# Sample attention: the value page becomes the stationary operand, 16 weight columns move, and all pages add up in one PSUM bank

## The chip, the cores and the metric

One core of a Trainium2 chip runs the whole kernel in one launch. The metric is the device time in microseconds, the median of several executions. All data is fp32; the large projections are made of three fp32r matmuls on split operands.

## What is computed

The kernel is one inference step of a two-layer decoder for a prompt of 512 tokens and for 8 samples of 4 new tokens each. Layer 0 is a recurrent block, layer 1 a stick-breaking attention block. For the samples the attention also reads 1,024 past positions, 8 pages of 128 for each sample, out of a paged pool:

```
past_v = cache_v[page_table].reshape(Bs, n_pages * PAGE_SIZE, KV_HEADS, HEAD_DIM)

z = einsum('bqkgd,bskd->bkgqs', qb, k) / sqrt(HEAD_DIM) + bias
mask = kpos[None, :] < qpos[:, None]
log_keep = where(mask, log_sigmoid(-z), 0.0)
suffix = cumsum(log_keep, axis=4, reverse=True) - log_keep
attn = where(mask, exp(log_sigmoid(z) + suffix), 0.0)
o = einsum('bkgqs,bskd->bqkgd', attn, v)
```

There are 16 query heads in 4 groups (KV_HEADS = 4), of 128 dimensions. So for one sample and one key head 16 columns (4 query heads by 4 tokens) meet a key page and a value page of 128 positions by 128 dimensions. The suffix sum runs backwards over positions, so pages are taken from the newest to the oldest.

## The kernel before

Five engines run programs of their own, written out in the order in which they execute, and meet at semaphores. TensorE's program is: transposes of the input, layer 0 (`block_a`, `pair_b`), the prompt's attention between the projections of layer 1 (`pair` with `qk`, `later`, `rest`, `pv`), then the sample attention, which is the stage of this change, and then the output projection (`pair_e`), whose first weights are loaded before the sample attention begins.

The sample attention goes in steps n = 0 to 8: step 0 is the new tokens themselves (keys `KST`, values `VST`), steps 1 to 8 are one page of each of the 8 samples. In step n TensorE does, in this order (`d_step`):

- for b = 0 to 7 (the sample), `d_turn` transposes the four heads of its key page into a bank of `PS` (L860), a copy by ACT (even b, L1205) or DVE (odd b, L1676) takes it to `KPT`, and four matmuls of 16 moving columns make the scores in `Z` (L878). The transposes run two or three samples ahead, so a step begins with 12 of them and ends with three samples' scores in a row;
- `d_values(n - 1)`: the values of the step before (L851). The weights of one sample (64 columns: 4 key heads by 16) are the stationary operand and the whole value page, 512 columns of 4 heads by 128 dimensions, moves. The result is 64 rows by 512 columns in bank `d_bank(b)` of `PS`. Each row meets all four heads, and only one in four of the blocks is wanted;
- `d_rest_keys(n - 1)` and `d_later_keys(n)`: 512-column matmuls with a triangle of ones, which carry the suffix sum in `later_sum` (L837, L838, L832, L833).

Meanwhile DVE and ACT turn the scores of step n into the exponent (`d_chain`, `d_exps`). DVE has another task in between: `add_values` adds each of the eight banks to an accumulator in SBUF (`value_sums`: `OA` for samples 0 to 5, two pieces of `T` for 6 and 7; L1632). POOL clears these accumulators ahead of the stage. Since key transposes and values share the four banks of `PS`, both wait for these adds (`d_sum_b`). After step 8, 32 transposes turn the accumulators (L900), and DVE multiplies the wanted blocks into the gate (L1684).

SP loads the pages, `KPG` and `VPG`, into two slots; a value slot is free when the matmuls that read it have ended (`d_pv_b`).

Of the kernel before, what the change touches and what calls it, by code (L numbers as in the profile page):

```python
# [26 lines left out]
ALU = mybir.AluOpType  # L27
# [6 lines left out]
NB, NT = 8, 4  # L34
# [10 lines left out]
DH = 128  # L45
NH, NKV, GRP = 16, 4, 4
KVW = NKV * DH
PAGE = 128
NPAGE = 8
# [53 lines left out]
def build(nc, a, out):  # L103
    ctx = ExitStack()
    with ctx:
        def sem(name):
            return ctx.enter_context(nc.semaphore(name))
# [4 lines left out]
        def sb(name, shape, dt=F32, offset=None):  # L112
            size = 4
            for n in shape[1:]:
                size *= n
            if offset is None:
                offset = at[0]
                at[0] += (size + 31) // 32 * 32
            return nc.alloc_sbuf_tensor_at(name, list(shape), dt, offset=offset), offset


        U, U_AT = sb("U", [P, 40, TOK], F32R)
        Y, Y_AT = sb("Y", [P, KR, TOK])
        raw, _ = sb("raw", [P, 2, UT, P])
        WS, _ = sb("WS", [P, 2, 2, UT, P], F32R)
        GW, GW_AT = sb("GW", [P, 2, 2, BLK])
        GWS, GWS_AT = sb("GWS", [P, 2, 2, 2, BLK], F32R)
        T, T_AT = sb("T", [P, 12, 572])
        RS, _ = sb("RS", [P, TOK])
        CH, _ = sb("CH", [P, KR, CROWS])  # L130
# [17 lines left out]
        VPG, _ = sb("VPG", [P, 2, NB, KVW], offset=U_AT + 2 * NB * KVW * 4)  # L148
        KPT, _ = sb("KPT", [P, 4, KVW], offset=U_AT + 4 * NB * KVW * 4)


        OA, _ = sb("OA", [NKV * GRP * NT, 6, KVW], offset=U_AT + (4 * NB + 4) * KVW * 4)

        YO, _ = sb("YO", [P, 5, D], offset=U_AT)

        xin, _ = sb("xin", [P, 5, D], offset=Y_AT)
# [59 lines left out]
        kp_odd = sem("kp_odd")  # L216
        kp_used = sem("kp_used")
        d_mask = sem("d_mask")
        d_cleared = sem("d_cleared")
        d_z = sem("d_z")  # L220
        d_zout = sem("d_zout")
        d_l = sem("d_l")
# [5 lines left out]
        d_rest = sem("d_rest")  # L228
        d_exp = sem("d_exp")
        d_at = sem("d_at")  # L230
        d_pv_b = sem("d_pv_b")
        d_sum_b = sem("d_sum_b")
        d_turned = sem("d_turned")
        d_out = sem("d_out")
        x_in = [sem(f"x_in{t}") for t in range(5)]
        rows_in = sem("rows_in")
# [43 lines left out]
        block = ctx.enter_context(nc.Block())  # L280

        QR = NKV * GRP * NT

        def value_sums(b):
            return OA[:, b, :] if b < 6 else T[0:QR, 5 if b == 6 else 8, 0:KVW]

        def d_columns(tile):

# [6 lines left out]
        def d_bank(b):  # L295

            return PS[:, b % 4 // 2, b % 2, :]
# [26 lines left out]
        def _(sp):  # L324
# [123 lines left out]
            def load_step(n, slot, reused):  # L448

                load_pages(n, slot, KPG, a["cache_k"], keys_in, (kp_t, n * 8 - 16) if reused else None)  # L450
                load_pages(n, slot, VPG, a["cache_v"], values_in, (d_pv_b, n * 8 - 8) if reused else None)

            load_step(1, 1, False)
            load_step(2, 0, False)
# [26 lines left out]
        def _(pool):  # L481
# [89 lines left out]
                ins = pool.affine_select(out=m8[:, k], in_=m8[:, k], compare_op=ALU.is_ge, fill=0.0, base=0,  # L571
                                         pattern=[[-NT, NB], [0, GRP], [0, NT]], channel_multiplier=1)
            ins.then_inc(d_mask, 1)

            pool.wait_ge(pv_done, NH * 4)
            pool.wait_ge(q_low, NH)
            pool.memset(OA[:], 0.0)
            for b in (6, 7):
                ins = pool.memset(value_sums(b), 0.0)
            ins.then_inc(d_cleared, 1)  # L580

            for n in range(2):
                add_square(3 * KD + n, n, 3, n == 0)
# [6 lines left out]
        def _(pe):  # L590
# [249 lines left out]
            def d_values(n, slot, pages=None):  # L840

                if isinstance(n, int) and n == 0:
                    pe.wait_ge(d_at, 1)
                else:
                    pe.wait_ge(d_exp, n + 1)
                    pe.wait_ge(values_in[slot], pages)
                for b in range(NB):
                    if b >= 4:
                        pe.wait_ge(d_sum_b, n * 8 + (b - 3))
                    v = VST[:, :] if isinstance(n, int) and n == 0 else VPG[:, slot, b, :]  # L850
                    ins = pe.matmul(d_bank(b)[0:QR, :], T[:, 4, b * QR:(b + 1) * QR], v, start=True, stop=True)  # L851
                    ins.then_inc(d_pv_b, 1)

            def d_turn(n, slot, b, first):
                if not first and b < 2:
                    pe.wait_ge(d_sum_b, n * 8 - 8)
                if not (first and b < 4):
                    pe.wait_ge(kp_odd if b % 2 else kp_even, n * 4 + (b // 2 - 5))
                for k in range(NKV):
                    ins = pe.transpose(d_bank(b)[:, k * P:(k + 1) * P], KPG[:, slot, b, k * DH:(k + 1) * DH], IDN[:])  # L860
                ins.then_inc(kp_t, 1)
# [31 lines left out]
                d_step(i * 2 + 1, 1, i * PAGES + PAGES, i * PAGES)  # L893
            d_step(NPAGE, 0, NPAGE // 2 * PAGES, NPAGE // 2 * PAGES)
            d_values(NPAGE, 0, NPAGE // 2 * PAGES)

            for b in range(NB):
                pe.wait_ge(d_sum_b, (NPAGE + 1) * NB)
                for k in range(NKV):
                    ins = pe.transpose(d_bank(k)[:, b * QR:(b + 1) * QR], value_sums(b)[:, k * DH:(k + 1) * DH], IDN[0:QR, 0:QR])  # L900
            ins.then_inc(d_turned, 1)


            def pair_e(i, first):
# [25 lines left out]
        def _(act):  # L930
# [248 lines left out]
            def d_exps(n, rows):  # L1179
                q = slice(0, SEQ)  # L1180
                act.wait_ge(d_zout, n + 1)
                if not (isinstance(n, int) and n == 0):
                    act.wait_ge(d_sp, n)
                steps.done(nc.scalar.activation(T[0:rows, 1, q], T[0:rows, 0, q], ACT.Abs))
                steps.done(nc.scalar.activation(T[0:rows, 1, q], T[0:rows, 1, q], ACT.Exp, scale=-1.0))
                nc.scalar.activation(T[0:rows, 1, q], T[0:rows, 1, q], ACT.Ln, bias=1.0).then_inc(d_l, 1)
                act.wait_ge(d_sp, n + 1)
                if isinstance(n, int) and n == 0:
                    act.wait_ge(pv_done, 64)
                else:  # L1190
                    act.wait_ge(d_rest, n)
                nc.scalar.activation(KVP[:, 0, :], T[:, 2, q], ACT.Copy).then_inc(d_high, 1)
                act.wait_ge(d_arg, n + 1)
                if not (isinstance(n, int) and n == 0):
                    act.wait_ge(d_pv_b, n * 8)
                nc.scalar.activation(d_weights(rows), d_columns(T[0:rows, 3, q]), ACT.Exp).then_inc(d_exp, 1)  # L1196

            d_exps(0, NS)
# [37 lines left out]
        def _(dve):  # L1236
# [388 lines left out]
            head_out(*last_head)  # L1625


            def add_values(m, sequences):

                for b in sequences:  # L1630
                    dve.wait_ge(d_pv_b, m * 8 + (b + 1))
                    V.tensor_tensor(value_sums(b), value_sums(b), d_bank(b)[0:QR, :], ALU.add).then_inc(d_sum_b, 1)  # L1632

            def d_chain(n, par, rows):
                q = slice(0, SEQ)
                fresh = isinstance(n, int) and n == 0
                if fresh:
                    dve.wait_ge(d_z, 1)
                else:
                    dve.wait_ge(kp_used, n * 8)  # L1640
                    dve.wait_ge(d_l, n)
                V.scalar_tensor_tensor(T[0:rows, 0, q], Z[0:rows, 0, par, :], SCALE, T[0:rows, 6, q],
                                       ALU.mult, ALU.add).then_inc(d_zout, 1)
                if not fresh:
                    add_values(n - 1, range(0, 4))
                dve.wait_ge(d_l, n + 1)
                steps.done(V.scalar_tensor_tensor(T[0:rows, 2, q], T[0:rows, 0, q], 0.0, T[0:rows, 1, q], ALU.max, ALU.add))
                if fresh:
                    steps.done(V.tensor_tensor(T[0:rows, 3, q], T[0:rows, 0, q], T[0:rows, 2, q], ALU.subtract))
                    dve.wait_ge(d_mask, 1)  # L1650
                    V.tensor_tensor(T[0:rows, 2, q], T[0:rows, 2, q], T[0:rows, 7, q], ALU.mult).then_inc(d_sp, 1)
                else:
                    V.tensor_tensor(T[0:rows, 3, q], T[0:rows, 0, q], T[0:rows, 2, q], ALU.subtract).then_inc(d_sp, 1)
                if not fresh:
                    add_values(n - 1, range(4, 5))
                dve.wait_ge(d_high, n + 1)
                V.tensor_tensor(KVP[:, 1, :], T[:, 2, q], KVP[:, 0, :].bitcast(F32), ALU.subtract).then_inc(d_low, 1)
                if not fresh:
                    add_values(n - 1, range(5, 8))
                dve.wait_ge(d_later, n + 1)  # L1660
                V.tensor_tensor(T[0:rows, 3, q], T[0:rows, 3, q], later_sum[0:rows, :], ALU.subtract).then_inc(d_arg, 1)
                if fresh:
                    dve.wait_ge(d_exp, 1)
                    V.tensor_tensor(d_weights(rows), d_weights(rows), d_columns(T[0:rows, 7, q]), ALU.mult).then_inc(d_at, 1)

            d_chain(0, 0, NS)
            dve.wait_ge(d_cleared, 1)
            with dve.Fori(0, NPAGE // 2) as i:
                steps.loop(i, 0, 2)
                for m in (1, 2):  # L1670
# [5 lines left out]
                        V.tensor_copy(KPT[:, b % 4, :], d_bank(b)).then_inc(kp_odd, 1)  # L1676
                    d_chain(n, m % 2, P)
            steps.leave(NPAGE // 2)
            add_values(NPAGE, range(NB))
            dve.wait_ge(d_turned, 1)  # L1680
            for k in range(NKV):
                y = Y[:, k * GRP:(k + 1) * GRP, SEQ:TOK].rearrange("p g (b t) -> p g b t", t=NT)
                o = d_bank(k).rearrange("p (b k g t) -> p k g b t", b=NB, k=NKV, g=GRP)[:, k]
                ins = V.tensor_tensor(y, y, o, ALU.mult)  # L1684
            ins.then_inc(d_out, 1)

# [56 lines left out]
```

## Time and profile before

| | |
|---|---|
| median of 3 runs | 2100.48 us (2094.29 to 2105.5) |
| profiled execution | span 2086.1 us; its own time is not among those listed |
| TensorE matmul busy | 1896.6 us, 91% of the span |
| DVE busy | 1143.1 us, 55% |
| ACT busy | 787.0 us, 38% |
| mean granted TensorE clock | 0.92 of full speed |
| from 1596 to 1840 us (sample attention but its start) | granted clock 0.75 on average |

The span runs from the first to the last instruction of the one execution that was profiled. The granted clock is a share of TensorE's full speed of 2.4 GHz; 0.50 is 1.2 GHz. Matmul records overlap, since they are pipelined: the mean duration of one is longer than the distance from one to the next, and it is the distance that adds up.

### The profile page before, as it was taken

The numbers are of one execution on the slowest core, as the hardware profiler recorded it, in microseconds if no ns is written. First come the engines' busy times: TensorE is split into PE (matmuls) and PEld (weight loads), VectorE is DVE, ScalarE is ACT, GpSimd is POOL, SyncE is SP. The second block draws the span as 40 slices with busy tenths as digits, with TensorE's granted clock in tenths as the row PEclk, the third lists the DMA queues.
The fourth block names the chain that finished last, engine by engine and source line by source line (L and its number), as shares of the span: only waits on it lengthen the run. The fifth ranks groups of instructions, "written<-read, shape, count | busy, mean of one in ns | idle before, by whom it ended". The sixth has DMA issues, their size and how long they took to land.

```text
span 2086.1 us, 35505 instructions
## 1 busy us (share of the span) xinstructions
PE 1896.6 (91%) x13482; PEld 1793.9 (86%) x13482; DVE 1143.1 (55%) x1880; ACT 787.0 (38%) x1132; POOL 274.1 (13%) x186
## 2 busy tenths in 40 slices
PE   4999999999979999658999999999986988989995
PEld 3999999999979999648989999999984766679993
DVE  4766666666664222584665675775775344352226
ACT  3244443444452222233554554554563111132222
POOL 4100000000000010243223222223220000001110
PEclk9999999999999999859999999999996677799995
DMA  5323233232212232342212222222225245313224
GB/s 194 94 85 90 81 90 90 81 90 85 86 55 77 86 90 85 124 135 82 67 57 83 71 61 83 72 61 82 70 81 164 77 129 160 97 41 90 82 92 150
DMA packets 278697, 191.50 MB, mean 92 GB/s; under 512 B 7899, under 2 KB 250715, under 8 KB 277979
## 3 DMA queue, kind: packets, MB, share of 16 engines
q1 hardware_dynamic: 277708, 188.03, 30.4%
q0 software_dynamic: 896, 2.23, 0.4%
q8 instruction: 59, 0.97, 0.2%
q14 instruction: 34, 0.28, 0.0%
HBM read 174.26 MB, written 15.97 MB: 91 GB/s over the span
## 4 chain that ended last, share of the span: by engine, by line
PE 76%; DVE 11%; ACT 6%; issue 5%; DMA 1%; POOL 0%; SPq 0%; ACTq 0%; DVEq 0%; POOLq 0%
PE PS L593 20%; PE PS L595 20%; PE PS L594 20%; PE Z L878 4%; PE PS L851 4%; PE PS L860 2%; PE Z L593 1%; PE Z L595 1%; PE Z L594 1%; DVE Y L1465 1%; ACT L1124 1%; DVE U L1528 1%; DMA prow<-in_state_h_dram 1%; DVE RS L1300 1%; DVE WS L1243 1%
## 5 line engine op out<-in xcount | busy, mean ns | idle before, releaser
L593 PE MATMUL PS<-U,WS 128*128 128x272 f32 x3712 | 1091.1, 294 | 59.3 <-DVE U L1472 34.2
L595 PE MATMUL PS<-U,WS 128*128 128x272 f32 x3712 | 1087.8, 293 | 0.0
L594 PE MATMUL PS<-U,WS 128*128 128x272 f32 x3712 | 1084.1, 292 | 0.0
L593 PEld LDWEIGHTS PS<-U,WS 128*128 128x128 f32 x3712 | 713.7, 192 | 66.4 <-issue 34.5
L594 PEld LDWEIGHTS PS<-U,WS 128*128 128x128 f32 x3712 | 713.9, 192 | 0.8
L595 PEld LDWEIGHTS PS<-U,WS 128*128 128x128 f32 x3712 | 714.0, 192 | 0.0
L1243 DVE TENSOR_TENSOR WS<-raw,WS 128x1024 fp32r<-128x1024 f32 (+1 forms) x240 | 302.4, 1260 | 502.7 <-ACT WS L939 500.2
L939 ACT ACTIVATE WS<-raw 128x1024 fp32r<-128x1024 f32 (+1 forms) x240 | 246.7, 1028 | 612.0 <-PE PS L595 608.6
L505 POOL TENSOR_TENSOR raw<-raw,GN 128x1024 f32<-128x1024 f32 x80 | 159.8, 1997 | 435.3 <-DMA raw<-in_b_w_in_dram 337.4
L517 POOL TENSOR_TENSOR T<-T 128x544 f32<-128x544 f32 x60 | 88.4, 1473 | 379.5 <-ACT T L1035 377.0
L514 POOL COPY T<-T 128x544 f32<-128x544 f32 x4 | 3.1, 787 | 902.3 <-ACT T L1035 875.5
L878 PEld LDWEIGHTS Z<-QS,KPT 128*128 128x128 f32 x512 | 94.4, 279 | 1.4 <-ACT KPT L1205 1.4
L878 PE MATMUL Z<-QS,KPT 128*128 128x16 f32 x512 | 91.8, 322 | 0.5
L851 PE MATMUL PS<-VPG,T 128*64 128x512 f32 x128 | 71.0, 718 | 2.3 <-ACT T L1196 2.3
L1518 DVE TENSOR_TENSOR T<-T,Z 128x256 f32<-128x256 f32 (+1 forms) x64 | 33.3, 521 | 60.6 <-PE Z L732 60.4
L1676 DVE COPY KPT<-PS 128x512 f32<-128x512 f32 x32 | 22.1, 691 | 73.4 <-PE PS L860 73.4
L851 PEld LDWEIGHTS PS<-VPG,T 128*64 128x64 f32 x128 | 20.3, 166 | 46.6 <-issue 43.6
L860 PE MATMUL PS<-IDN,KPG 128*128 128x128 f32 x256 | 52.2, 355 | 8.0 <-DVE T L1632 8.0
L1035 ACT ACTIVATE T<-Y 128x544 f32<-128x544 f32 (+1 forms) x48 | 31.1, 648 | 71.6 <-DVE Y L1443 71.6
L1070 ACT ACTIVATE T<-T 128x256 f32<-128x256 f32 (+1 forms) x64 | 31.7, 496 | 69.7 <-DVE T L1491 69.7
L1088 ACT ACTIVATE U<-T 128x256 fp32r<-128x256 f32 (+1 forms) x64 | 31.7, 495 | 58.0 <-DVE T L1523 58.0
L1098 ACT ACTIVATE U<-T 128x256 fp32r<-128x256 f32 (+1 forms) x64 | 31.9, 499 | 56.6 <-DVE T L1507 56.6
(216 smaller groups left out, 2078.4 us busy)
## 6 DMA issues: line engine op xcount, KB each, us to landing
raw<-in_a_w_in_dram SPq DMA_DIRECT2D x80, 512.0 KB, 3.8
raw<-in_b_w_in_dram SPq DMA_DIRECT2D x64, 512.0 KB, 4.0
raw<-in_a_w_out_dram SPq DMA_DIRECT2D x32, 512.0 KB, 3.8
raw<-in_b_w_out_dram SPq DMA_DIRECT2D x32, 512.0 KB, 3.8
KPG<-in_cache_k_dram SPq DMA_DIRECT2D x64, 256.0 KB, 2.9
VPG<-in_cache_v_dram SPq DMA_DIRECT2D x64, 256.0 KB, 2.9
T<-scratch_x SPq DMA_DIRECT2D x32, 272.0 KB, 2.9
scratch_x<-T SPq DMA_DIRECT2D x16, 272.0 KB, 2.1
```

The lines of the kernel that those rows point to most:

```text
L505: pool.tensor_tensor(raw[:, slot], raw[:, slot], g, ALU.mult).then_inc(w_fold, 1)
L517: ins = pool.tensor_tensor(T[:, 6, 0:TOK], T[:, 6, 0:TOK], sq, ALU.add)
L593: pe.matmul(psum, w_hi, x_hi, start=first, stop=False)
L594: pe.matmul(psum, w_hi, x_lo, start=False, stop=False)
L595: return pe.matmul(psum, w_lo, x_hi, start=False, stop=last)
L851: ins = pe.matmul(d_bank(b)[0:QR, :], T[:, 4, b * QR:(b + 1) * QR], v, start=True, stop=True)
L860: ins = pe.transpose(d_bank(b)[:, k * P:(k + 1) * P], KPG[:, slot, b, k * DH:(k + 1) * DH], IDN[:])
L878: ins = pe.matmul(zs[:, slot, cols], KPT[:, b % 4, k * DH:(k + 1) * DH], QS[:, cols], start=True, stop=True)
L939: nc.scalar.activation(WS[:, slot, 0, 0:tiles, :], raw[:, slot, 0:tiles, :], ACT.Copy).then_inc(w_high, 1)
L1098: nc.scalar.activation(U[:, 36, q], T[:, 2, q], ACT.Copy).then_inc(sp_high, 1)
L1243: V.tensor_tensor(WS[:, slot, 1, 0:tiles, :], raw[:, slot, 0:tiles, :], WS[:, slot, 0, 0:tiles, :].bitcast(F32), ALU.subtract).then_inc(w_ ...
L1518: V.tensor_tensor(T[:, 3, q], T[:, 3, q], later_sum[:, q], ALU.subtract).then_inc(arg_ready, 1)
```

## The change

The operands of the sample's value matmuls change places. The value page of one key head (128 positions by 128 dimensions) is now the stationary operand, and the 16 weight columns of that head move. The result, 128 dimensions by 16 columns, comes out as the gate needs it, so the transposes at the end go. All samples and all pages add up in one PSUM bank, `o_sum`, which the prompt's attention used before (hence the new wait for `o_out`, once). With it go the accumulators, their clearing on POOL, the adds on DVE, and the waits for them. A value slot is now free after the last of a stretch's matmuls, counted by one semaphore for the stretch.

```diff
-        OA, _ = sb("OA", [NKV * GRP * NT, 6, KVW], offset=U_AT + (4 * NB + 4) * KVW * 4)
...
-        def value_sums(b):
-            return OA[:, b, :] if b < 6 else T[0:QR, 5 if b == 6 else 8, 0:KVW]
...
-                load_pages(n, slot, VPG, a["cache_v"], values_in, (d_pv_b, n * 8 - 8) if reused else None)
+                load_pages(n, slot, VPG, a["cache_v"], values_in, (d_values_done, n - 1) if reused else None)
...
-            pool.memset(OA[:], 0.0)
-            for b in (6, 7):
-                ins = pool.memset(value_sums(b), 0.0)
-            ins.then_inc(d_cleared, 1)
...
+                fresh = isinstance(n, int) and n == 0
+                if fresh:
+                    pe.wait_ge(o_out, NH)
                 for b in range(NB):
-                    if b >= 4:
-                        pe.wait_ge(d_sum_b, n * 8 + (b - 3))
-                    v = VST[:, :] if isinstance(n, int) and n == 0 else VPG[:, slot, b, :]
-                    ins = pe.matmul(d_bank(b)[0:QR, :], T[:, 4, b * QR:(b + 1) * QR], v, start=True, stop=True)
-                    ins.then_inc(d_pv_b, 1)
+                    v = VST[:, :] if fresh else VPG[:, slot, b, :]
+                    for k in range(NKV):
+                        cols = slice(b * QR + k * 16, b * QR + k * 16 + 16)
+                        ins = pe.matmul(o_sum[:, cols], v[:, k * DH:(k + 1) * DH], T[:, 4, cols],
+                                        start=fresh and b == 0 and k == 0, stop=False, skip_group_check=True)
+                ins.then_inc(d_values_done, 1)
 
             def d_turn(n, slot, b, first):
-                if not first and b < 2:
-                    pe.wait_ge(d_sum_b, n * 8 - 8)
...
-            for b in range(NB):
-                pe.wait_ge(d_sum_b, (NPAGE + 1) * NB)
-                for k in range(NKV):
-                    ins = pe.transpose(d_bank(k)[:, b * QR:(b + 1) * QR], value_sums(b)[:, k * DH:(k + 1) * DH], IDN[0:QR, 0:QR])
-            ins.then_inc(d_turned, 1)
...
-                    act.wait_ge(d_pv_b, n * 8)
+                    act.wait_ge(d_values_done, n)
...
-            def add_values(m, sequences):
-
-                for b in sequences:
-                    dve.wait_ge(d_pv_b, m * 8 + (b + 1))
-                    V.tensor_tensor(value_sums(b), value_sums(b), d_bank(b)[0:QR, :], ALU.add).then_inc(d_sum_b, 1)
-
...
-                if not fresh:
-                    add_values(n - 1, range(0, 4))
...
-                if not fresh:
-                    add_values(n - 1, range(4, 5))
...
-                if not fresh:
-                    add_values(n - 1, range(5, 8))
...
-            add_values(NPAGE, range(NB))
-            dve.wait_ge(d_turned, 1)
+            dve.wait_ge(d_values_done, NPAGE + 1)
...
-                o = d_bank(k).rearrange("p (b k g t) -> p k g b t", b=NB, k=NKV, g=GRP)[:, k]
+                o = o_sum.rearrange("p (b k g t) -> p k g b t", b=NB, k=NKV, g=GRP)[:, k]
```

On TensorE, this is the program before from the last scores of a page step, through the values, to the first transposes of the next step. Rows are matmuls with their output, operands and shape, and waits in brackets; a matmul here is two records of the trace where it is fp32 and no transpose.

```order
L878 MATMUL Z<-QS,KPT 128x16 x3
L851 MATMUL PS<-VPG,T 64x512 [waits values_in1,d_exp]
L851 MATMUL PS<-VPG,T 64x512 x3
L851 MATMUL PS<-VPG,T 64x512 [waits d_sum_b]
L837 MATMUL Z<-KVP,TRI 128x512 [waits d_arg]
L838 MATMUL Z<-KVP,TRI 128x512
L832 MATMUL Z<-KVP,TRI 128x512 [waits d_arg,d_low]
L833 MATMUL Z<-KVP,TRI 128x512
L858 ISA [waits d_sum_b]
L860 MATMUL PS<-IDN,KPG 128x128 [waits kp_even]
```

The row that waits for `d_sum_b` stands four times, for samples 4 to 7. The same place on TensorE in the changed program (its lines are numbered anew: L864 are the scores, L838 the values, L816 to L822 the sums, L846 the transposes):

```order
L864 MATMUL Z<-QS,KPT 128x16 x3
L838 MATMUL Z<-T,VPG 128x16 [waits values_in1,d_exp]
L838 MATMUL Z<-T,VPG 128x16 x31
L821 MATMUL Z<-KVP,TRI 128x512 [waits d_arg]
L822 MATMUL Z<-KVP,TRI 128x512
L816 MATMUL Z<-KVP,TRI 128x512 [waits d_arg,d_low]
L817 MATMUL Z<-KVP,TRI 128x512
L846 MATMUL PS<-IDN,KPG 128x128 [waits kp_even]
```

Eight matmuls of 512 moving columns have become 32 of 16, and neither they nor the transposes behind the sums wait for DVE any more. On DVE, this is the program before over one step of the loop, from the scores to the exponent:

```order
L1642 SCALAR_TENSOR_TENSOR T<-Z,T 128x512 [waits d_l,kp_used]
L1632 TENSOR_TENSOR OA<-OA,PS 64x512 [waits d_pv_b]
L1647 SCALAR_TENSOR_TENSOR T<-T 128x512 [waits d_l]
L1653 TENSOR_TENSOR T<-T 128x512 [waits dve_step]
L1657 TENSOR_TENSOR KVP<-T,KVP 128x512 [waits d_high]
L1632 TENSOR_TENSOR T<-T,PS 64x512 [waits d_pv_b]
L1661 TENSOR_TENSOR T<-T,Z 128x512 [waits d_later]
```

Of L1632 there are four adds ahead of L1647, one behind L1653 and three ahead of L1661. The changed program on DVE at the same place:

```order
L1616 SCALAR_TENSOR_TENSOR T<-Z,T 128x512 [waits d_l,kp_used]
L1619 SCALAR_TENSOR_TENSOR T<-T 128x512 [waits d_l]
L1625 TENSOR_TENSOR T<-T 128x512 [waits dve_step]
L1627 TENSOR_TENSOR KVP<-T,KVP 128x512 [waits d_high]
L1629 TENSOR_TENSOR T<-T,Z 128x512 [waits d_later]
```

The eight adds are gone and nothing has moved otherwise.

## Rows read from the trace of the kernel before

**Rows 1.** The page: granted TensorE clock, in tenths, 40 equal slices.

```profile
PEclk9999999999999999859999999999996677799995
```

**Rows 2.** Chain that ended last, in order of time: start us, us, what.

```profile
1595.29 0.80 PE Z L832
...
1608.29 7.01 PE PS L851 x16
...
1638.85 9.48 PE PS L851 x16
...
1668.50 8.31 PE PS L851 x16
...
1700.45 9.40 PE PS L851 x16
...
1730.10 9.93 PE PS L851 x16
...
1748.55 0.80 PE Z L878 x8
...
1752.40 2.59 PE Z L878 x24
...
1766.02 2.25 PE PS L860 x12
...
1780.54 4.93 PE Z L878 x24
1785.47 9.55 PE PS L851 x16
...
1815.13 8.38 PE PS L851 x16
...
1828.72 8.46 PE PS L851 x16
...
1837.94 2.23 PE PS L900 x32
```

**Rows 3.** Windows, TensorE: stretch, its us, PE busy (records), granted clock, DMA.

```profile
1599.50:1619.80 20.30, 17.67 (x106) 1.00 0.36 105
...
1643.90:1657.30 13.40, 10.63 (x58) 1.00 0.40 117
...
1671.20:1681.20 10.00, 7.37 (x21) 1.00 0.23 71
...
1705.30:1718.80 13.50, 10.73 (x58) 1.00 0.48 135
...
1736.00:1766.60 30.60, 25.20 (x135) 1.00 0.55 163
1766.80:1790.40 23.60, 23.60 (x97) 0.50 0.48 144
1790.60:1804.10 13.50, 10.71 (x59) 1.00 0.46 132
...
1818.00:1828.00 10.00, 6.91 (x17) 1.00 0.00 0
...
1831.60:1841.60 10.00, 7.78 (x45) 1.00 0.00 0
1841.80:1848.50 6.70, 5.83 (x26) 0.50 0.00 0
```

**Rows 4.** The page, value matmuls: busy, mean ns; idle before, releaser.

```profile
L851 PE MATMUL PS<-VPG,T 128*64 128x512 f32 x128 | 71.0, 718 | 2.3 <-ACT T L1196 2.3
```

**Rows 5.** Line L1632 by itself: durations ns; who waited, us, times.

```profile
L1632 DVE TENSOR_TENSOR OA<-OA,PS x54: 670/678/681, 1609.3 to 1835.5; 64x512 f32<-64x512 f32 x54
...
  PE PS L860: 8.0, 7
```

**Rows 6.** Timeline of one seam: start us, us, engine, line, operation, count.

```profile
1709.78 0.50 PE L837 MATMUL Z<-KVP,TRI 128*128 128x512 f32 x1
...
1713.87 1.53 PE L860 MATMUL PS<-IDN,KPG 128*128 128x128 f32 x12 [1.12 <-DVE T L1632]
```

More of the change, by code:

```diff
@@ L218, in build @@
         d_mask = sem("d_mask")
-        d_cleared = sem("d_cleared")
         d_z = sem("d_z")
@@ L230, in build @@
         d_at = sem("d_at")
-        d_pv_b = sem("d_pv_b")
-        d_sum_b = sem("d_sum_b")
-        d_turned = sem("d_turned")
+        d_values_done = sem("d_values_done")
         d_out = sem("d_out")
@@ L573, in _ @@
             ins.then_inc(d_mask, 1)
-            pool.wait_ge(pv_done, NH * 4)
-            pool.wait_ge(q_low, NH)
-            pool.memset(OA[:], 0.0)
-            for b in (6, 7):
-                ins = pool.memset(value_sums(b), 0.0)
-            ins.then_inc(d_cleared, 1)
             for n in range(2):
@@ L1666, in _ @@
             d_chain(0, 0, NS)
-            dve.wait_ge(d_cleared, 1)
             with dve.Fori(0, NPAGE // 2) as i:
```

## Prediction

> **What bounds the kernel now.** The first view to read is the page: TensorE is busy over most of the span, and its granted clock reads 9 in tenths nearly everywhere, but 6 or 7 in five of the slices that cover the sample attention [rows 1]. The change lies inside those slices, so the next view is the chain of work that ended last, in order of time [rows 2]. From 1608.29 us, where the first value stretch starts, to 1840.19 us (1837.94 plus the transposes behind it), it is almost all TensorE: transposes of key pages (L860), score matmuls of 16 columns (L878), value matmuls (L851), with DVE at the seams. That is 231.9 us, and the sum below is made against it. One page step reads so: 12 transposes at 1766.02, five groups of 8 score matmuls with 4 transposes between them, then 24 score matmuls at 1780.54, and the value stretch at 1785.47. (The trace has two matmul records for one fp32 matmul of the program; I count records, 24 being 12 matmuls.)
>
> The third view gives the granted clock of the stretches between its changes [rows 3]. It has two levels, 1.2 and 2.4 GHz (0.50 and 1.00). Laid beside the chain it shows a pattern. The clock fell among transposes and score matmuls: at 1657.4, 1681.3, 1718.9, 1766.7 and 1804.2. In the seven value stretches that began at half clock it rose each time, 2.6 to 5.9 us behind their start: 1638.85 to 1643.9, 1668.50 to 1671.2, 1700.45 to 1705.3, 1730.10 to 1736.0, 1785.47 to 1790.6, 1815.13 to 1818.0, 1828.72 to 1831.6. So the 512-column value matmuls are what gives the clock back; the stretch of 24 score matmuls, busy without a gap by the profile, never did.
>
> The fourth view is the list of groups by line: 128 value records at a mean of 718 ns over both clocks, and DVE adds of 0.68 us, 54 of them into OA and, for two samples of eight, 18 into T [rows 4, 5]. The adds hide behind TensorE but for one place: the transposes of the next page wait for the last add, 1.12 us in the step shown and 8.0 us over seven steps [rows 5, 6].
>
> **The change part by part.** *Value matmuls.* 16 records of 512 columns with 64 columns loaded become 64 records (8 samples, 4 heads, 2 records each) of 16 columns with 128 columns loaded. The trace has exactly this shape in L878: 24 records in 2.59 us at full clock, 108 ns each, and 24 in 4.93 us at half, 205 ns each [rows 2]. A value stretch therefore costs 64 x 108 = 6.9 us at full clock and 64 x 205 = 13.1 us at half. The old one took 7.0 at full clock and 8.3 to 9.9 where it began at half. So at full clock the edit is even, and everything hangs on the clock. The operands lie in other buffers than those of L878; I take the same price, since both the load and the moving columns have its shape.
>
> *The clock.* The new stretch is more of what L878 is, and under L878 the clock fell and never rose. I take it that the clock falls in or before each value stretch and doesn't rise there. Two places remain that could lift it. One is the pair of 512-column sums with the 12 transposes behind it. In the kernel before they stand apart by the 1.12 us wait; after the change nothing parts them. The same form stands once in the trace, ahead of page step 1: sums at 1595.29, transposes until the first scores, and the clock rose at 1599.4 [rows 2, 3]. At half clock that stretch lasts about 3.2 us (12 transposes in 2.25 us, and two sums). Of the seven rises in old value stretches three came within 3.2 us of the start (2.7, 2.9 and 2.9 us) and four later. So I take 3 of the 7 later steps to rise there. A rise there lets the rest of the scores run at full clock: five groups at 1.28 instead of 2.45 us ((1752.40 - 1748.55) / 3, and (1780.54 - 1766.02 - 2.25) / 5) save 5.9 us, and the last 24 records 2.3 us, together 8 us. It is as little as 4 if the clock falls again midway, as at 1718.9, and 10 if it lasts into the values.
>
> *DVE adds and what they held up.* Gone are 72 adds; the 1.12 us wait goes in about seven steps, and no other work takes its place: the copies of keys on ACT then come behind the exponent of the step, hidden by 12 transposes at half clock; at full clock some 0.4 us of it would show. At the end the last add, the 32 transposes (L900) and the wait for them go, 3 us from the end of the values (1828.72 + 8.46) to 1840.19.
>
> *POOL, buffers, queues.* The memsets of the accumulator lie under the end of the prompt attention, and nothing waits for them. SP issues the same page loads; the value slot is freed at the end of the stretch as before, a whole step ahead of its next use. Nothing.
>
> *The sum, all at half clock.* Values of step 0: between 6.9 and 13.1, I take 10. Values of 1 to 8: 8 x 13.1 = 105. Seven times scores with transposes, 1766.02 to 1785.47, 19.45 us, and the seam: before, 1709.85 to 1713.87, 4.0 us, less the 1.1 us wait, plus about 0.8 us for four sums at half clock (0.50 against 0.80 us for the first of a pair [rows 2, 6]): 3.7. That is 7 x 23.15 = 162. The last seam, with the exponent in it, was 5.2 (1823.51 to 1828.72) and becomes 6.0. In all 283 us against 232: +51. With three rises of 8 us: +27. The matmuls behind the stage began at half clock already (the last row of [rows 3]), so nothing is added there. The profiled execution's span is 2086.1 us, 14.4 below the median of the runs shown, 2100.5; its own time is not listed. I carry the difference over: 2113 for the span, 2128 for the median.
>
> *A rule against the trace.* The last 24 score records kept TensorE busy without an idle gap, and seven times the clock was still at half when the values began [rows 2, 3]. The Trainium skill (TensorE: Matmul & The Clock Gate, Part 1, and its closing table) says that sustained work releases the clock and that idle gaps between bursts lose it. The rows speak against reading "busy" so; the rule is the third rival's. The same page (Part 4) says that transposes don't count as busy for the clock. By that the sums and transposes would lift nothing, and the sum would stay +51; the one row of this form, 1599.4, speaks against it.
>
> **The rivals.** *First, no rises:* the sums and transposes lift the clock in none or one of the steps. For it: only one place of this form is in the trace, and four of seven rises took longer than the stretch lasts. Time: +43 to +51, 2143 to 2152. Chance 0.27.
>
> *Second, many rises:* it rises in five to seven steps, if what counts is that nothing parts the sums from the transposes. 51 - 5 x 8 = +11, down to -5: 2096 to 2112. Chance 0.11, of it 0.09 within 0.5%.
>
> *Third, the other side:* loading 128 columns for every record counts as work for the clock, and it behaves as before or better. As before: a stretch starts at half clock, 4.1 us on average to the rise is 20 records, 44 more at 108 ns are 4.8 us, 8.9 in all as now; the wait (7 x 1.1) and the end (3) are gained, -11: 2090. Held at full clock all through, as the skill's rule on continuous work has it: nine stretches of 6.9, seven of 10.5 + 2.9, the last seam 5.2, make 161 us, -71: 2030. It decides as soon as value stretches rise of themselves. Against it: L878 loads as much for each record and lifted nothing. Chances 0.07 and 0.04.
>
> *The forecast:* two to four rises of 6 to 9 us: 2115 to 2140. Chance 0.51.
>
> **How the numbers follow.** 2128 is the likeliest. Leaving out the third rival and the edge of the second, the range is 2106 to 2152. A measurement of this kernel tells about 0.5%, 10.5 us: faster beyond it 0.10 (third rival, most of it, and little of the second), within it 0.12, slower 0.78 (the forecast and the first rival).
>
> **What would show it.** In the changed kernel the records of the value line should come every 205 ns with the clock at 0.50, 13.1 us a stretch in most of the steps, no rise inside one; the rises that exist should lie at the end of the 12 transposes; those transposes should follow the sums with no wait for DVE; the stage from 1596 on should be some 25 to 50 us longer, and the rest of the kernel unchanged. A value stretch that ends at full clock having begun at half would prove the forecast wrong, and so would records that don't halve their pace with the clock.

## The result, and the profile after

The changed kernel takes 2122.88 us (median of 4 runs, 2117.94 to 2127.64) against 2097.39 us for the kernel before (4 runs, 2091.62 to 2105.5): ratio 1.0128, 95% interval 1.0087 to 1.0169, or 25.5 us slower. The forecast was 2128, slower.

The page of the changed kernel shows where to look. This is the granted TensorE clock in tenths, 40 equal slices, to be laid beside [rows 1]:

```profile
PEclk9999999999989999769999999999976555579995
```

Around the sample attention the slices read 7, 6, 5, 5, 5, 5, 7, where the kernel before had 6, 6, 7, 7, 7 and no 5. The rest is much as it was. Next, windows of TensorE (stretch, its us, busy, records, clock, DMA). First the kernel before:

```profile
1608.30:1840.20 231.90, 208.30 (x880) 0.74 0.38 112
```

and then the changed kernel, with the same stretch of the program (first value matmul to the gate's multiply), its rises, and one value stretch:

```profile
1620.50:1622.70 2.20, 2.20 (x12) 0.50 0.00 0
1622.90:1626.10 3.20, 3.20 (x33) 1.00 0.00 0
1626.30:1656.80 30.50, 29.00 (x133) 0.50 0.11 36
1657.00:1660.20 3.20, 3.20 (x33) 1.00 0.77 230
...
1637.10:1650.80 13.70, 13.70 (x66) 0.50 0.00 0
1604.40:1874.30 269.90, 256.39 (x1280) 0.55 0.32 97
```

The stage went from 231.9 to 269.9 us, and its clock from 0.74 to 0.55. Outside it nothing moved: 2086.1 - 231.9 = 1854 us before, 2120.5 - 269.9 = 1851 us after. So the change is the stage's. The profiles differ by 38 us there and the medians by 25.5, mainly because the first profile of before was an execution some 10 us below the median; against a second one (below), with 240.5 us, the stage is 29.4 us longer.

The chain that ended last, of the changed kernel, answers to [rows 2]. L864 are the scores, L838 the values, L846 the transposes, L821 a sum:

```profile
1604.38 12.34 PE Z L838 x64
...
1620.49 2.48 PE PS L846 x12
1622.97 0.80 PE Z L864 x8
...
1627.29 1.52 PE Z L864 x8
...
1632.20 4.93 PE Z L864 x24
1637.13 13.65 PE Z L838 x64
1650.78 0.61 PE Z L821
...
1654.55 2.52 PE PS L846 x12
...
1671.20 13.65 PE Z L838 x64
...
1860.43 13.85 PE Z L838 x64
```

A value stretch is 64 records in 13.65 us, 213 ns each, seven times over, with step 0 at 12.34 and step 8 at 13.85: 121.7 us in all, where the kernel before took 77.5 (the eight stretches of [rows 2], and one of 7.01). Against these +44.2 us everything else in the stage gave back 6.2. The groups of 8 scores behind the transposes take 0.80 us, those later in a step 1.52: here the clock rose, at the end of the 12 transposes, and fell again 3.4 us later. It did so in all seven steps, 34.07 us apart (1637.13 to 1671.20), so the seven are hardly seven independent trials.

The seam, from the timeline of the changed kernel, against [rows 6]:

```profile
1688.00 0.63 PE L817 MATMUL Z<-KVP,TRI 128*128 128x512 f32 x1
...
1688.42 2.75 PE L846 MATMUL PS<-IDN,KPG 128*128 128x128 f32 x12
```

The transposes follow the last sum with no wait for DVE.

### The profile page after: what moved, and what is told of

Same layout as the page of the kernel before. It is cut to its first block, busy times and chain, and to the rows that moved or that the text cites. A ratio compares the mean times of both kernels' runs of the same rounds, so it can differ in the third digit from the quotient of the medians.

```text
span 2120.5 us, 36122 instructions
## 1 busy us (share of the span) xinstructions
PE 1942.0 (92%) x13882; PEld 1894.1 (89%) x13882; DVE 1096.7 (52%) x1808; ACT 786.7 (37%) x1132; POOL 271.2 (13%) x183
## 4 chain that ended last, share of the span: by engine, by line
PE 78%; DVE 10%; ACT 5%; issue 5%; DMA 1%; POOL 0%; SPq 0%; ACTq 0%; DVEq 0%; POOLq 0%
PE PS L577 19%; PE PS L579 19%; PE PS L578 19%; PE Z L838 6%; PE Z L864 4%; PE PS L846 2%; PE Z L577 1%; PE Z L578 1%; PE Z L579 1%; DVE Y L1445 1%; ACT L1104 1%; DMA prow<-in_state_h_dram 1%; DVE T L1487 1%; DVE RS L1280 1%; DVE U L1508 1%
## 5 line engine op out<-in xcount | busy, mean ns | idle before, releaser
L577 PE MATMUL PS<-U,WS 128*128 128x272 f32 x3712 | 1090.6, 294 | 59.5 <-DVE U L1452 34.1
L838 PEld LDWEIGHTS Z<-T,VPG 128*128 128x128 f32 x512 | 110.1, 333 | 2.2 <-ACT T L1176 2.2
L838 PE MATMUL Z<-T,VPG 128*128 128x16 f32 x512 | 110.5, 374 | 1.4 <-ACT T L1176 1.4
L864 PEld LDWEIGHTS Z<-QS,KPT 128*128 128x128 f32 x512 | 91.8, 273 | 0.0
L864 PE MATMUL Z<-QS,KPT 128*128 128x16 f32 x512 | 88.6, 315 | 0.0
L846 PE MATMUL PS<-IDN,KPG 128*128 128x128 f32 x256 | 56.5, 379 | 0.0
```

Of the source, the lines that this page charges most:

```text
L577: pe.matmul(psum, w_hi, x_hi, start=first, stop=False)
L838: ins = pe.matmul(o_sum[:, cols], v[:, k * DH:(k + 1) * DH], T[:, 4, cols], start=fresh and b == 0 and k == 0, stop=False, skip_group_chec ...
L864: ins = pe.matmul(zs[:, slot, cols], KPT[:, b % 4, k * DH:(k + 1) * DH], QS[:, cols], start=True, stop=True)
```

## The experiments

Each run's ratio is its time over that of the kernel before, timed in the same group of runs, with the 95% interval in brackets. The text set off in each was written ahead of the run.

**The kernel before once more.** No edit.

> The kernel before, unchanged, for a second profile. The stretch from the first value matmuls to the gate's multiply was 231.9 us in the first profile. Theory: where the clock falls and rises differs from execution to execution, so this stretch comes out anywhere from 230 to 255 us, and value stretches take 7.0 us at full clock or 8.3 to 10 us where they begin at half. Rival (the places are fixed by the program): the same rises and falls, within 2 us of 231.9.

Window, and two rows of the chain, of this second execution:

```profile
1605.40:1845.90 240.50, 216.89 (x881) 0.72 0.37 108
```

```profile
1634.16 8.46 PE PS L851 x16
...
1695.77 8.38 PE PS L851 x16
```

240.5 us against 231.9, with the clock up and down at other places, so the places are not fixed by the program. Every value stretch that began at half clock ended at full, as in the first profile.

**The changed kernel once more**, timed with others.

> The changed kernel, unchanged, for a second profile and its time beside the others of this group. In the first one the clock rose at the end of the transposes in seven of seven steps and each time fell 3.4 us later, scores with transposes took 16.7 us, values 13.65 us, and from the first values to the gate's multiply it was 269.9 us. Theory (whether the short run of sums and transposes lifts the clock is chance): here fewer steps have a rise, steps without one take 2.8 us more, the stretch comes out at 268 to 284 us, and no rise lies inside a value stretch. Rival (the program fixes the rises): seven again, 270 us within 1.

Ratio 1.0118 (1.0065 to 1.0171), 2123.72 us; the profiled run was its slowest, 2137.76. Chain of this execution:

```profile
1633.29 2.56 PE PS L846 x12
...
1648.12 4.93 PE Z L864 x24
1653.05 13.65 PE Z L838 x64
1670.47 2.56 PE PS L846 x12
...
1744.83 2.29 PE PS L846 x12
1753.53 2.59 PE Z L864 x24
1756.12 12.78 PE Z L838 x64
1772.67 2.56 PE PS L846 x12
```

Two steps of seven had a rise, again at the end of the transposes, and there the clock stayed at full for 10.2 us, through all the scores. Such a step is 1744.83 to 1772.67, 27.8 us; one without is 1633.29 to 1670.47, 37.2 us. The stage was 274.3 us. The theory holds: seven short rises that save 37.2 - 34.1 = 3.1 us each, or two long ones that save 9.3, come to about the same. The execution took 15.6 us more than the first, and only 4.4 of them lie in the stage. Another 8.0 lie just ahead of it: the first sums and transposes (ahead of page step 1, where the change leaves TensorE's program as it was) lifted the clock in the first profile and not in this one. So from those transposes to the first values it was 11.7 us there and 19.8 here.

**A gap between sums and transposes.**

```diff
                 d_rest_keys(n - 1)
                 d_later_keys(n)
+                pe.wait_ge(d_exp, n + 1)
```

> The changed kernel, in which TensorE waits, behind the sums of each page step, for the exponent of that step before it begins the next transposes, some 1.5 us of idling in each of eight steps. In the changed kernel the clock rose in seven of seven steps at the end of the transposes that follow the sums at once. Theory (it is the unbroken run of sums and transposes that lifts it): those rises vanish, scores with transposes go back from 16.7 to 19.5 us, and the stage becomes 7 x (1.5 + 2.8) = 30 us longer, ratio to the kernel before about 1.027. Rival (the transposes alone, or the time since the last rise, lift it): the rises stay, and only the idling is added, 11 us, ratio 1.018.

Ratio 1.0308 (1.0246 to 1.0370), 2163.15 us. Window and timeline:

```profile
1562.00:1927.00 365.00, 319.57 (x1431) 0.50 0.31 92
```

```profile
1709.64 0.63 PE L817 MATMUL Z<-KVP,TRI 128*128 128x512 f32 x1
...
1712.38 1.97 PE L846 MATMUL PS<-IDN,KPG 128*128 128x128 f32 x8 [2.11 <-ACT T L1177]
```

```profile
1653.69 13.65 PE Z L838 x64
...
1692.85 13.65 PE Z L838 x64
```

Not one rise. The edit puts 2.3 us between sums and transposes in this step (2.7 us from the start of the last sum to the transposes, against 0.4), and a step is 39.2 us, in two steps 39.5, against 37.2 without rise and without gap: about 15 us in seven steps. The stage is 307.7 us, 38 and 33 above the two profiles of the changed kernel, so the lost rises (22 and 19 us) make up the rest. The other executions agree: the granted clock over the whole kernel was 0.877 to 0.884 in all four, and 0.888 to 0.899 in the eight of the changed kernel. So it is the run of sums and transposes together that can lift the clock; here 2.8 us of transposes alone did not.

That it can does not mean that it will. The same closed seam lifted the clock in seven of seven steps of one profile of the changed kernel and in two of seven of the other, as with 64 moving columns (below). And ahead of page step 1, where sums and transposes follow each other without a gap in all thirteen profiles of this case, the clock rose in eight and not in five; the kernel with the gap is one of the five.

**128 moving columns.** The value matmuls move the columns of two samples past one head's values; sample outputs are not the reference's.

```diff
+                        wide = slice(b // 2 * 128, b // 2 * 128 + 128)
-                        ins = pe.matmul(o_sum[:, cols], v[:, k * DH:(k + 1) * DH], T[:, 4, cols],
+                        ins = pe.matmul(o_sum[:, wide], v[:, k * DH:(k + 1) * DH], T[:, 4, wide],
```

> The changed kernel with 128 moving columns in each value matmul in place of 16 (the columns of two samples, all meeting one head's values, so the sample outputs are not the reference's): the same 64 records and the same 64 loads of 128 columns a stretch, eight times the moving columns. Theory (the value stretch is long because the clock stays at half under it): the clock rises inside the stretch, which falls from 13.65 to 8.5 to 10.5 us, the scores behind it begin at full clock as in the kernel before, and the kernel is faster than the changed one by 25 to 40 us, about level with the kernel before. Rival (the price of a record is that of loading 128 columns, whatever the clock, or grows with what moves): 13.65 us a stretch or more, and the time of the changed kernel or longer.

Ratio 0.9857 (0.9798 to 0.9916), 2066.98 us: eight times the moving columns, and some 55 us less than the changed kernel. Windows and chain (L839 are its values):

```profile
1618.00:1819.90 201.90, 184.34 (x1281) 0.82 0.42 127
1692.40:1698.00 5.60, 5.60 (x27) 0.50 0.19 56
1698.20:1715.10 16.90, 14.78 (x129) 1.00 0.49 153
```

```profile
1666.01 7.24 PE Z L839 x64
...
1692.57 9.96 PE Z L839 x64
```

The clock rises within a stretch that begins at half clock, and the stretch takes 9.96 us; one that keeps full clock takes 7.24, 113 ns a record with the same load of 128 columns. The rival on the price of the load is out. The gain was larger than I expected, because scores and seams kept the clock too.

**64 moving columns**, all four heads of one sample past one head's values; sample outputs are not the reference's. The edit is the same with 64 for the last 128.

> The changed kernel with 64 moving columns in each value matmul in place of 16 (columns of all four heads meeting one head's values, so the sample outputs are not the reference's). With 128 it was 56 us faster than the changed kernel. Theory: 64 columns at half clock still hide behind the load of 128, so a record costs 213 ns as with 16, and what differs is only whether the clock rises: between nothing (2123 us, as with 16) and the 56 us of the 128 (2067). I expect no rise inside a stretch, but that a clock which is at full when the stretch begins stays there longer, and the time in the lower part, 2100 to 2123. Rival (time grows with the columns that move): slower than the changed kernel.

Ratio 1.0155 (1.0093 to 1.0217), 2135.05 us: from the changed kernel's 1.0118 and 1.0128 it can't be told. Chain:

```profile
1689.12 13.73 PE Z L839 x64
1717.72 13.00 PE Z L839 x64
```

No rise inside a stretch; a record costs what it does with 16 columns (13.73 us a stretch against 13.65). The hoped-for advantage of a clock that stays up longer did not come: it rose in two steps, for 10.2 us each, as in the second profile of the changed kernel.

**Without the adds.** In the kernel before `add_values` returns at once, and TensorE's waits for it go (ahead of the last transposes it waits for the cleared accumulators instead); sample outputs are not the reference's.

```diff
                 for b in sequences:
-                    dve.wait_ge(d_pv_b, m * 8 + (b + 1))
-                    V.tensor_tensor(value_sums(b), value_sums(b), d_bank(b)[0:QR, :], ALU.add).then_inc(d_sum_b, 1)
+                return
...
-                    if b >= 4:
-                        pe.wait_ge(d_sum_b, n * 8 + (b - 3))
...
-                if not first and b < 2:
-                    pe.wait_ge(d_sum_b, n * 8 - 8)
```

> The kernel before without its 72 DVE adds and without the waits for them (the pages' values then never reach the accumulators, so the sample outputs are not the reference's). It is one part of the change alone, with the value matmuls as they were. Theory (the adds hide but for the 1.1 us wait in seven steps and 0.7 us at the end): 8.5 us faster than the kernel before, and a little more where sums and transposes without a gap lift the clock in a step that it had left at half: 8 to 20 us, ratio 0.990 to 0.996. Rival (the DVE work held up much more than that, and its loss should have been a gain of the change): 25 us or more. Rival (it hid entirely): no difference.

Ratio 0.9866 (0.9823 to 0.9908), 2069.06 us: 28 us faster: beyond my 8 to 20, and in the range of the first rival. Window of its stage:

```profile
1604.00:1810.10 206.10, 188.57 (x880) 0.81 0.42 126
```

The clock was 0.81 over the stage against 0.74 and 0.72 (this execution was 12 us below the median of its kernel). About 8 us of waits gone don't make 28; the remainder is clock. The windows give its size: at 0.81, 2 x 0.19 x 206.1 = 78 us of the stage were at half clock, in the kernel before 121 and 135. So 42 or 56 us fewer were at half clock, which at double the clock is a gain of 21 or 28; with the 8 us of waits this estimate makes 29 or 36, where the stages differ by 25.8 and 34.4. It leaves nothing for the adds to have held up besides.

**Additional matmuls in the kernel before**, to test the clock by itself. Their operands are resident, their result goes to a score bank that is free, and nobody reads it. For that bank to be free, TensorE waits at the start of a step until DVE has read the scores of the step before (`d_zout`, n for n - 1), and once for the resident weights (`w_low`); these waits, which the cut below leaves out, are in all five kernels with additional matmuls.

```diff
+            def warm(slot, count):
+                for _ in range(count):
+                    pe.matmul(zs[:, 1 - slot, :], TRI[:, 0, :], warm_w, start=True, stop=True, skip_group_check=True)
...
                     ins.then_inc(kp_used, 1)
+                    warm(slot, 1 if b < 5 else 2)
...
                 d_rest_keys(n - 1)
+                warm(slot, 5)
                 d_later_keys(n)
+                warm(slot, 3)
```

> The kernel before with additional matmuls of 512 columns whose result nobody reads: 1 behind the scores of samples 0 to 4, 2 behind those of 5 to 7, 5 between the two pairs of sums, 3 behind the second pair, 19 a step. At full clock they add 11 x 0.21 = 2.3 us a step to the path, the other 8 lie in waits. Theory (the stage is long because the clock falls among the scores): the clock stays at full through the stage; a step is 10.5 + 2.3 us of scores, 7.0 of values, 4.0 of seam, 24 us against 29.5 on average, and the kernel is 35 to 50 us faster, ratio 0.976 to 0.983. Rival (the clock falls in spite of them): 19 more matmuls at 0.21 to 0.43 us, 20 to 50 us slower.

Ratio 0.9815 (0.9750 to 0.9881), 2054.87 us. Windows and chain (L857 are its values, L828 the additional ones):

```profile
1604.60:1649.90 45.30, 43.47 (x261) 1.00 0.34 98
1650.10:1653.30 3.20, 3.20 (x5) 0.50 0.59 188
1653.50:1701.10 47.60, 45.76 (x266) 1.00 0.55 163
```

```profile
1613.53 1.06 PE Z L885 x8
1614.60 0.33 PE Z L828
...
1625.69 7.01 PE PS L857 x16
```

152 matmuls more, and 40 us less. From the first values on, the clock fell only for 3.4 us at a time (6.8 behind the last), once in two steps.

**Only in the seams of the kernel before**: the 5 and the 3, none among the scores.

> The kernel before with five additional matmuls of 512 columns between the two pairs of sums and three behind the second pair, all of which lie in waits of TensorE for DVE; all adds and waits are kept. Theory (the kernel without the adds was 28 us faster because the clock was then less often at half among the scores): most of that gain comes with the adds in place, 10 to 28 us, ratio 0.987 to 0.995. Rival (the adds and their waits cost the time themselves): no change within 5 us.

Ratio 0.9873 (0.9813 to 0.9934), 2064.55 us. Its adds and waits are all there, and it is level with the kernel without adds (0.9866). Its stage is 207.5 us at a clock of 0.84, where the kernel without the adds had 206.1 at 0.81. So a gain of the size that came without the adds can be had with every add in place, through the clock.

**Additional matmuls in the changed kernel, in its values too:** 5 in the seam, 1 or 2 behind the scores, and in the values:

```diff
                         ins = pe.matmul(o_sum[:, cols], v[:, k * DH:(k + 1) * DH], T[:, 4, cols],
                                         start=fresh and b == 0 and k == 0, stop=False, skip_group_check=True)
+                    if warmed is not None and b < 7:
+                        warm(warmed, 2)
```

> The changed kernel with additional matmuls of 512 columns whose result nobody reads: as in the kernel before with its 19, but none behind the second pair of sums, where nothing waits any more, and 14 in each value stretch, two behind each of the first seven samples. Theory (at full clock the swapped value matmuls cost 108 ns a record and the swap is even but for the waits that it saves): the clock stays at full nearly all through; a value stretch is 64 x 0.108 + 14 x 0.21 = 9.9 us, a seam 2.9 us, the end 3 us shorter; against the kernel before with additional matmuls that is 8 x 2.9 more for the 14, 7 x 1.1 and 3 less, so 10 to 15 us slower than it and 50 to 60 us faster than the changed kernel: ratio to the kernel before 0.983 to 0.990. Rival (a record of the swapped form costs 213 ns at either clock): a value stretch is 16 us or more, and the time is above that of the kernel before.

A miss: ratio 1.0213 (1.0146 to 1.0280), 2130.86 us, with single runs from 2105.95 to 2157.83; even the fastest is above every run of the kernel before in this group. Chain of that fastest one (L844 are its values, L812 the additional ones):

```profile
1608.83 0.80 PE Z L844 x8
...
1612.38 1.04 PE Z L812 x2
1613.42 1.52 PE Z L844 x8
...
1804.38 0.80 PE Z L844 x8
1805.18 0.56 PE Z L812 x2
```

At full clock 8 records of the swapped form take 0.80 us, no more than the scores. But two additional matmuls to 8 records held the clock only at times. It fell within five of the eight value stretches that have them, and then the 14 cost twice as much each (1.04 us for two in place of 0.56). Three kept full clock, as the one at 1804.38, and took 10.3 us, near the 9.9 expected. So the price was right and the assumption about the clock wrong.

**Additional matmuls in the changed kernel, in the seam only** (5 a step).

> The changed kernel with five additional matmuls of 512 columns, whose result nobody reads, between the two pairs of sums of each step, where TensorE waits 1.5 us for DVE. They make the run of 512-column matmuls ahead of and into the transposes longer; nothing else differs. Theory (a longer unbroken run of sums and transposes lifts the clock in every step): seven steps of about 28 us, like the two with a rise in the second profile of the changed kernel (27.8 us), in place of 37.2 us without one; 0.6 us a step is lost where five at half clock outlast the wait. The kernel is 30 to 45 us faster than the changed one, ratio to the kernel before 0.99 to 1.00. Values still take 13 us. Rival (the rises come by chance, whatever stands there): as the changed kernel, or 4 us slower.

Ratio 1.0033 (1.0002 to 1.0064), 2103.54 us, about 20 us faster than the changed kernel; I expected 30 to 45. Windows:

```profile
1642.90:1656.70 13.80, 13.80 (x66) 0.50 0.00 0
1659.60:1669.60 10.00, 9.38 (x84) 1.00 0.74 237
```

The clock rose in seven of seven steps, for 10.2 us in five of them and 6.8 in two, and each time it was at half again when the values began, which take 13.65 us. (Ahead of the last stretch it rose once more, for 3.4 us, and that stretch took 11.80.) The direction is the theory's, and the rival of chance does not fit: all ten executions are below the fastest of the changed kernel (2105.55 the slowest, against 2112.52). A step is 29.0 to 32.8 us rather than 28, since the rise came now earlier, now later among transposes and scores.

**The same, and among the scores too.**

> The changed kernel with the five additional matmuls between the pairs of sums and with 1 behind the scores of samples 0 to 4 and 2 behind those of 5 to 7, none in the values. Theory: scores at full clock throughout, and a clock that is still at full when the values begin falls within them, so a value stretch takes 10 to 13.6 us. The additional matmuls of the scores cost 2.3 us a step and give back 1 to 3 us of the values: level with the kernel that has only the five, within 10 us. Rival (held up so long the clock lasts through the values as well): 7 us a stretch, 25 us faster than with the five alone.

Ratio 1.0027 (0.9998 to 1.0057), 2098.90 us, level with the seam alone. Chain:

```profile
1670.26 9.93 PE Z L844 x64
1698.53 13.47 PE Z L844 x64
1729.68 11.22 PE Z L844 x64
```

What the values gain, the additional matmuls cost, as expected; the rival's 25 us did not come.

## Why the prediction was right

*The mechanism.* It said that the swap is even at full clock, that the new value stretch neither lifts nor holds the clock, and that the old one was what lifted it. All three are shown. Even at full clock: 0.80 us for 8 records (the miss above), and 7.24 us a stretch with 128 columns, against 7.01; no run had all 64 records of 16 columns at full clock with nothing between them. No rise under it: none inside a value stretch in either profile of the changed kernel, nor with 64 columns. And the loss is the clock's: taking out the adds gains 28 us (0.9866), the swap on top of that loses about 55 (1.0128), and the same swap with enough moving columns to lift the clock loses nothing beyond noise (0.9857).

*The values.* I priced a record at 205 ns from the groups of 24 scores; it measured 213, 13.65 us a stretch instead of 13.1. Step 0 was 12.3, not 10. In all 121.7 us against a term of 115. (In the second profile step 0 began at half clock and took 13.65.)

*The seam and the scores.* Seams 3.8 us (1650.78 to 1654.55), taken as 3.7; scores with transposes at half clock 19.76 (1633.29 to 1653.05), taken as 19.45; a whole step without a rise 37.2 against 36.25. The 0.3 us in the scores are a misreading: I took 2.25 us for 12 transposes at half clock from a place that had full clock for its first 0.6 us ([rows 3], to 1766.60), and at half throughout they take 2.56. The last seam was 5.2, taken as 6.0.

*The rises* were the uncertain term: 3 of 7 steps at 8 us, 24 us. It measured 7 at 3.1 in one execution, 22, and 2 at 9.3 in the other, 19. The product was near, the factors were not: 3 steps and 8 us match neither profile, and they vary from one execution to the next, so that the product came out is in part luck. The place was right, at the end of the 12 transposes, and the run with the gap shows that they need the closed seam.

*The number.* The forecast stage was 232 + 27 = 259 us, and it measured 269.9 and 274.3: the terms above were 11 to 15 us short, most of it in the values. That the median still came out 5 us below the forecast and not above it is luck. I added 14.4 us for the distance of the profiled span from the median, which belonged to one fast execution of the kernel before; the changed kernel's profiled execution had a time 1.7 us above its span and lay at the median. Span against span it was 2113 forecast and 2120.5 measured.

*The adds.* Their removal was taken as 7 x 1.1 + 3 us plus the rises. In the old form their removal is worth 28 us, more than I gave it even in the expectation of that run: I had counted the wait and not all that it did to the clock.

*The rivals.* The first (no rises) did not occur in the profiles of the changed kernel. The second had its seven rises in one profile, but short ones, so the time was not its. The third is refuted: 128 loaded columns a record lifted nothing. The Trainium skill (TensorE: Matmul & The Clock Gate, Part 1, and its closing table) has sustained work release the clock; the trace disagrees, 13.65 us without a gap at 0.50. The Trainium skill (TensorE: Matmul & The Clock Gate, Part 4) has transposes not count as busy for the clock; the traces speak against it, as the same sums lifted the clock with transposes right behind them (seven, two and two times of seven) and never in seven with idling there. No run shows transposes lifting it by themselves.

*What is open.* Why the same closed seam lifts the clock in one step and not in another, and why a rise lasts 3.4 us in one execution and 10.2 in another with the same instructions behind it, I can't say; nor did I find a cheap way to hold the clock through swapped values that leaves nothing of the computation out. Between 64 moving columns, which lifted nothing, and 128, which did, no run looked.

## What to carry to other kernels

Price a matmul edit at both clocks, and ask what the edited matmuls did for the clock of everything around them: the old value matmuls did three quarters useless work and paid for themselves by lifting the clock for the scores. A short wait between two dense stretches can cost several times its length in this way (here 8 us of waits stood for 28), so fill it: 8 additional matmuls a step in the waits made the kernel before 1.3% faster, and 19 a step 1.9%. That is the fastest of all that leave nothing out, though the two intervals overlap. And when the clock moves from one execution to the next, compare many runs, and take a profile twice before a term of it is believed.

## What the runs showed of the hardware that was not expected

The same 64 loads and 64 matmuls a stretch took 13.65 us with 16 moving columns and 7.24 to 10.01 us with 128: more work in each matmul was faster. Two 512-column matmuls to every 8 small records held the clock among the last scores but through only three of eight stretches of values. And TensorE can be at half clock for 365 us on end while it is busy for 320 of them.
